# Two attention mixers: a fill piece ahead of the scores, rotary swaps on ScalarE, output pieces in halves

## The reference, cut to what matters

```python
proj = xn @ w_in                      # q, k, v: 12 heads of 64; qm: 4 memory heads; layer 0 also f_logit
log_f = log_sigmoid(f_logit + b_forget)                        # layer 0
sc = q @ k.T * scale + cumsum(log_f)[q] - cumsum(log_f)[k]     # layer 0, causal

x1, x2 = split(x, 2, axis=-1)                                  # layer 1, q and k of each head
y = concatenate([x1 * cos - x2 * sin, x2 * cos + x1 * sin])    # rotary embedding
# layer 1: three dilated branches, joined by their log-sum-exp

mem_out = softmax(qm @ km.T * scale) @ vm                      # 4 heads over 256 memory tokens
h = h + merge_heads([mix, mem_out]) @ w_out
```

## Time and profile before

| what | value |
|---|---|
| median of 3 runs | 1809.51 us (1806.91 to 1810.58) |
| the profiled execution | 1806.99 us |
| its span in the trace | 1805.2 us |
| TensorE busy | 1759.5 us, 97% |
| VectorE, ScalarE, GpSimd busy | 940.4, 533.6, 1015.1 us |

### The profile page before, as it was taken

One profiled execution on the slowest core, in us unless ns is written; L12 is line 12 of the kernel. 1 busy time (PEld: TensorE's weight loads), 2 busy tenths in 40 slices (PEclk: granted clock), 3 DMA queues, 4 the chain that ended last, 5 costly groups with the idle time before them and its releaser, 6 DMA issues.

```text
span 1805.2 us, 24432 instructions
## 1 busy us (share of the span) xinstructions
PE 1759.5 (97%) x9567; PEld 1404.3 (78%) x9572; DVE 940.4 (52%) x1896; ACT 533.6 (30%) x1183; POOL 1015.1 (56%) x1046
## 2 busy tenths in 40 slices
PE   7999999999989999999999999999999999999998
PEld 6886678676668967779888888887677888888886
DVE  5976754695543355533663166335765356415642
ACT  3614534312542344423220012023664211101111
POOL 7533375554237744335777677756434577677762
PEclk9989999999999999999999999999999999999999
DMA  5220312230233321113332333222111233233331
GB/s 177 82 77 19 117 59 94 77 99 29 71 105 106 94 71 50 69 47 90 106 98 88 95 99 104 88 94 71 49 69 48 70 94 114 96 93 94 95 103 47
DMA packets 170994, 151.16 MB, mean 84 GB/s; under 512 B 5192, under 2 KB 145992, under 8 KB 170880
## 3 DMA queue, kind: packets, MB, share of 16 engines
q1 hardware_dynamic: 169280, 148.12, 26.8%
q10 hardware_dynamic: 1600, 1.48, 0.3%
HBM read 147.45 MB, written 2.14 MB: 83 GB/s over the span
## 4 chain that ended last, share of the span: by engine, by line
PE 93%; DVE 4%; ACT 2%; issue 1%; another core or an unknown queue 0%; DMA 0%; ACTq 0%; DVEq 0%
PE ps L281 77%; PE ps L1989 3%; PE ps L2022 2%; PE ps L2007 2%; PE ps L352 1%; PE ps L640 1%; PE ps L1486 1%; PE ps L1464 1%; PE ps L1995 1%; PE ps L1407 1%; PE ps L1415 1%; PE ps L665 1%; PE ps L1423 0%; PE ps L672 0%; PE ps L1476 0%
## 5 line engine op out<-in xcount | busy, mean ns | idle before, releaser
L127 POOL TENSOR_SCALAR w_hi<-w_raw 128x512 fp32r<-128x512 f32 x520 | 315.7, 635 | 747.0 <-PE ps L281 742.3
L131 POOL TENSOR_TENSOR w_lo<-w_raw,w_hi 128x512 fp32r<-128x512 f32 x520 | 694.5, 1367 | 11.3
L281 PE MATMUL ps<-x_hi,w_hi 128*128 128x512 f32 (+1 forms) x1448 | 538.0, 372 | 0.7 <-DVE x_lo L434 0.7
L281 PE MATMUL ps<-x_hi,w_lo 128*128 128x512 f32 (+1 forms) x1448 | 527.9, 365 | 0.0
L281 PE MATMUL ps<-x_lo,w_hi 128*128 128x512 f32 (+1 forms) x1448 | 527.9, 365 | 0.0
L281 PEld LDWEIGHTS ps<-x_hi,w_hi 128*128 128x128 f32 x1448 | 274.8, 190 | 69.0 <-issue 19.8
L281 PEld LDWEIGHTS ps<-x_hi,w_lo 128*128 128x128 f32 x1448 | 274.8, 190 | 43.7
L281 PEld LDWEIGHTS ps<-x_lo,w_hi 128*128 128x128 f32 x1448 | 275.1, 190 | 40.8 <-issue 0.5
L2291 DVE SCALAR_TENSOR_TENSOR ffn_cv<-ps,col,ffn_cv 128x510 f32<-128x510 f32 (+1 forms) x176 | 131.8, 749 | 192.3 <-ACT ffn_cv L2269 187.6
L2269 ACT ACTIVATE ffn_cv<-ps,col 128x512 f32<-128x512 f32 x88 | 63.8, 775 | 500.2 <-PE ps L281 500.2
L309 DVE TENSOR_TENSOR h<-h,ps 128x512 f32<-128x512 f32 x64 | 43.9, 687 | 261.4 <-PE ps L281 261.3
(11 more groups left out here) (346 smaller groups left out, 2394.1 us busy)
## 6 DMA issues: line engine op xcount, KB each, us to landing
w_raw<-w_up SPq DMA_DIRECT2D x88, 512.0 KB, 5.0
w_raw<-w_down SPq DMA_DIRECT2D x16, 1024.0 KB, 5.0
w_raw<-od_w_in SPq DMA_DIRECT2D x12, 1024.0 KB, 5.2
w_raw<-w_in_fox SPq DMA_DIRECT2D x10, 1024.0 KB, 5.3
w_raw<-w_in_dil SPq DMA_DIRECT2D x10, 1024.0 KB, 5.1
w_raw<-w_out SPq DMA_DIRECT2D x8, 1024.0 KB, 5.0
w_raw<-ev_w_in SPq DMA_DIRECT2D x7, 1024.0 KB, 5.3
w_raw<-w_down SPq DMA_DIRECT2D x8, 768.0 KB, 4.5
```

What stands on the lines that cost most here:

```text
L127: ins = pool.tensor_scalar(hi[:, c:min(c + PIECE, size)], raw[:, c:min(c + PIECE, size)], 1.0, 1.0, ALU.mult, ALU.mult)
L131: ins = pool.tensor_tensor(lo[:, c:min(c + PIECE, size)], raw[:, c:min(c + PIECE, size)], hi[:, c:min(c + PIECE, size)].bitcast(F32), ALU. ...
L281: mm = pe.matmul(o, l, r, start=start and i == 0, stop=stop and i == 2)
```

## The change

- Each fill piece runs one step earlier. Piece 0 runs ahead of step 0: in layer 0 before scores(0), in layer 1 behind scores(0). Ropes 4 to 11 and the evacuations of fill blocks move one step with them.
- The four swaps by TensorE in layer 1 and their permutation table are gone, with the table's load. ScalarE makes these swaps too. Behind the evacuations of blocks 1 to 4 it copies the rows of q0, k0, q1 and k1 from SBUF to bank 5.
- The first output parts of tiles 0 and 1, four k each in steps 28 and 29, are cut into halves of two k, in steps 27, 28, 29 and 30.

```diff
-                                step = [f[0] for f in self.fill].index(m) + 2
+                                step = [f[0] for f in self.fill].index(m) + 1
...
-                    for dst, src in ((self.cos, "c_rope_cos"), (self.sin, "c_rope_sin"), (self.swap, "c_rope_swap"),
-                                     (self.mask, "c_dilated")):
+                    for dst, src in ((self.cos, "c_rope_cos"), (self.sin, "c_rope_sin"), (self.mask, "c_dilated")):
...
             def tensor(self, pe):
-                def swap(i):
-                    dst, tile, m = self.rope_tiles[i]
-                    if i == 0:
-                        pe.wait_ge(self.tables_in, 64)
-                    pe.wait_ge(self.evacuated.s, self.evacuated.at(max(m, 1) + 1))
-                    if i >= 1:
-                        pe.wait_ge(self.swap_free, i)
-                    pe.matmul(ps[:, 5, :], self.swap[:, :], dst[:, tile, :], start=True, stop=True).then_inc(self.swapped, 1)
...
                 for m in range(4, self.prelude):
                     self.dense(pe, m, 0, KD)
-                    if layer == 1:
-                        swap(m - 4)
+                if layer == 0:
+                    self.dense(pe, *self.fill[0])
                 scores(0)
+                if layer == 1:
+                    self.dense(pe, *self.fill[0])
                 for s in range(self.N):
                     if s + 1 < self.N:
                         scores(s + 1)
-                    if s < len(self.fill):
-                        self.dense(pe, *self.fill[s])
-                    elif s == self.N - 4:
+                    if s + 1 < len(self.fill):
+                        self.dense(pe, *self.fill[s + 1])
+                    elif s == self.N - 5:
                         pe.wait_ge(W.split_done, out_.slots[0][0] + 1)
                         pe.wait_ge(self.freed.s, self.freed.at(6))
                         pe.wait_ge(self.evacuated.s, self.evacuated.at(len(self.blocks) - 1))
-                        out_.part(pe, 0, 0, 0)
+                        out_.part(pe, 0, 0, 0, (0, 1))
+                    elif s == self.N - 4:
+                        out_.part(pe, 0, 0, 0, (2, 3))
                     elif s == self.N - 3:
                         pe.wait_ge(self.evacuated.s, self.evacuated.at(len(self.blocks)))
-                        out_.part(pe, 0, 0, 1)
+                        out_.part(pe, 0, 0, 1, (0, 1))
+                    elif s == self.N - 2:
+                        out_.part(pe, 0, 0, 1, (2, 3))
...
             def scalar(self, act):
+                def swap(i, x):
+                    if i >= 1:
+                        act.wait_ge(self.swap_free, i)
+                    for q in range(4):
+                        ins = act.activation(ps[32 * q:32 * q + 32, 5, :], x[32 * (q ^ 1):32 * (q ^ 1) + 32, :], ACT.Copy,
+                                             scale=1.0 if q % 2 else -1.0)
+                    ins.then_inc(self.swapped, 1)
...
                 for m in range(self.prelude):
                     evacuate(m)
+                    if self.layer == 1 and 1 <= m < 5:
+                        dst, tile, made = self.rope_tiles[m - 1]
+                        act.wait_ge(self.evacuated.s, self.evacuated.at(max(made, 1) + 1))
+                        swap(m - 1, dst[:, tile, :])
                 probs(0)
...
-                    if s < len(self.fill) and self.fill[s][2] == KD:
-                        evacuate(self.fill[s][0])
+                    if s + 1 < len(self.fill) and self.fill[s + 1][2] == KD:
+                        evacuate(self.fill[s + 1][0])
                     copy(s)
...
             def vector(self, dve):
-                    if i < 4:
-                        dve.wait_ge(self.swapped, i + 1)
-                    else:
-                        dve.wait_ge(self.act_swapped, i - 3)
-                        dve.wait_ge(self.evacuated.s, self.evacuated.at(m + 1))
+                    dve.wait_ge(self.swapped, i + 1)
+                    dve.wait_ge(self.evacuated.s, self.evacuated.at(m + 1))
```

More of the change, by code:

```diff
@@ L1839, in __init__ @@
                     self.tmp, self.mask = at("rope_tmp", 44, [P, 2, S]), at("dilated_mask", 72, [P, S])
-                    self.cos, self.sin, self.swap = at("rope_cos", 74, [P, S]), at("rope_sin", 76, [P, S]), at("rope_swap", 78, [P, P])
-                    self.tables_in, self.swapped, self.act_swapped, self.swap_free, self.roped = (
-                        sem(n) for n in ("rope_in", "swapped", "act_swapped", "swap_free", "roped"))
+                    self.cos, self.sin = at("rope_cos", 74, [P, S]), at("rope_sin", 76, [P, S])
+                    self.tables_in, self.swapped, self.swap_free, self.roped = (sem(n) for n in ("rope_in", "swapped", "swap_free", "roped"))
                 n = 2 * self.N
@@ L2080, in evacuate @@
                         if m in self.turned_by_act:
[L2081 to L2085, removed]
+                            swap(self.turned_by_act[m], ps[:, bank, :])
                         act.activation(dst, ps[:, bank, 0:dst.shape[1]], ACT.Copy).then_inc(self.evacuated.s, 1)
@@ L2179, in vector @@
                 else:
-                    dve.wait_ge(self.tables_in, 64)
+                    dve.wait_ge(self.tables_in, 48)
                     for i in range(4):
@@ L2475, in constants @@
     cos, sin = (np.tile(g(ang).astype(f).T, (4, 1)) for g in (np.cos, np.sin))
-    swap = np.zeros((P, P), f)
-    for m in range(P):
-        swap[m + 32 if m % 64 < 32 else m - 32, m] = -1 if m % 64 < 32 else 1
     time4 = np.tile(np.arange(0, S, 4, dtype=f)[None, :], (P, 1))
@@ L2482, in constants @@
             "c_rope_cos": np.ascontiguousarray(cos), "c_rope_sin": np.ascontiguousarray(sin),
-            "c_rope_swap": swap, "c_time4": time4, "c_ident": np.eye(P, dtype=f)}
+            "c_time4": time4, "c_ident": np.eye(P, dtype=f)}
 def layouts(a):
```

## The result

The changed kernel takes 1795.04 us (median of 6 runs, 1791.04 to 1796.91), the kernel before 1809.02 (6 runs, 1806.91 to 1810.58): a ratio of 0.9921, 95% interval 0.9907 to 0.9935, so 14.0 us less where 9.3 were forecast, and outside the stated range. The changed kernel's profiled execution took 1796.79, 10.2 less than that of before. Most of this document is about the 4 us between these two distances: the profiled execution of before was 2.0 under the median of its kernel, that of the changed kernel 1.75 over its own.

What follows compares the result with a forecast made beforehand. TensorE, busy 97% of the span, was taken as the bound, so its work and waits count. 2.24 + 6.15 + 1.3 - 0.4 = 9.3 us, so 1809.5 - 9.3 = 1800.2, range over all cases 1796.5 to 1805.

Steps and rivals of the forecast that it cites:

- The granted clock is not in question: Layer 1's stretch with the longest wait, 1240.5 to 1244, has clock 1.00, the upper level; no gain by the clock counted.
- the profiled execution lay 2.5 below the median: Profiled execution 1806.99 against median 1809.5; the predicted time was taken from the median, 1809.5 - 9.3.
- Part 1: Layer 0: fill piece 0 ahead of scores(0) removes their wait for the forget sums; gain 2.24 us.
- Part 2: Layer 1's prelude: four swaps leave TensorE (3.45) and the wait for logits(0) goes (2.70); gain 6.15 us.
- The exclusive lock: Layer 1's ropes wait for whole GpSimd operations: rope 4.5, loss 2.1, 1802.3 us; chance 0.04 within the late-rope rival's 0.12.
- Part 3: Ropes 4 to 11 and evacuations one step earlier: cost 0; 2.8 us if a GpSimd split ran then.
- Part 4: Mixer ends, output parts in halves: gain 0.70 in layer 1, 0.6 in layer 0; 0.4 lost to four piece changes.
- all four: Rivals: late ropes 1801.1-1804.3 (0.12); joined steps or halves fail 1801.5-1803 (0.09); slow swaps 1814.5 (0.03); only swaps gained 1806 (0.03).

Runs made afterwards that it cites:

- e6: Kernel before with the fill one step earlier in layer 0 alone; swaps, layer 1 and whole output parts as before: 1805.26 us, ratio 0.9975.
- e4: Changed kernel with layer 1's first four swaps put back on TensorE as matmuls: 1797.92 us, ratio 0.9938 against the kernel before.
- e3: Changed kernel with the output parts of tiles 0 and 1 whole again: 1798.41 us, ratio 0.9936 against the kernel before.
- e1: Kernel before under a new name, no edit: 1808.33 us over 12 runs, ratio 0.9988.
- e7: Kernel before with only the first four swaps moved to ScalarE, fill and output parts as before: 1803.62 us, ratio 0.9976.
- e11: Changed kernel with fill piece 0 behind scores(0) in layer 0 too, bringing back the wait for cum: 1798.52 us, ratio 0.9949 against the kernel before.
- e12: Kernel before once more, unchanged, on the same chip as later runs of the changed kernel: 1808.71 us, ratio 0.9997.

## Why the prediction was wrong

- **The step that failed is the first: "The granted clock is not in question".** It rested on the earlier trace rows, one execution. That profile was the exception: of the three of the unchanged program it is the only one in which the clock fell in neither mixer. Filling the waits, with no work saved, is worth 3.3 us in the means (92 unchanged runs 1808.7, 23 with idle work 1805.5); the changed kernel's 17 runs have 1795.6. So the whole, 13.2, is about 3 by the clock and 10 by work and waits. The split is an estimate over chips: within the two groups that have both kernels, idle work was worth 3.7 and 2.4. The mixers, 10.2, agree with it, and so do the runs at one mean clock, 0.994: unchanged and changed are 10.5 apart (1807.0 and 1796.6).
- **Chance has a share in the 14.0.** The six runs behind it had a mean of 1794.7, three of them at a mean clock of 0.996 or 0.997; the changed kernel's eleven later runs have 1796.0, with medians of 1796.74 and 1795.48. The first of these lies within the forecast's range, the second a little outside. Since the clock fell in the mixers of none of its three profiles, their scatter most likely comes from outside the mixers.
- **A sign of it was in the text.** I noted that the profiled execution lay 2.5 below the median and carried it along as a constant. It was no constant: the profile was a fast execution, and what made it fast was in reach of the change.
- **Part 1** had 2.24; layer 0's mixer lost 2.29 with that part alone (e6). Right.
- **Part 2** had 3.45 and 2.70. The swaps are worth 3.42 (e4). What is left of layer 1's 7.02 after them and the 1.01 of the halves is 2.59. Right; the chain of swaps and ropes ended 1.4 ahead instead of 1.0. The exclusive lock of the Trainium skill ("SBUF — State Buffer", "SBUF: two separate sides") would have made a rope of 4.5; the four took 2.4 to 3.75, so operations were held up, the longest, 1.67 instead of 0.68, by 0.99, but none by the full 1.27.
- **Part 3**, cost nothing: TensorE has no wait in steps 5 to 24.
- **Part 4** is the mis-sized term: 1.3 less 0.4 was forecast, 1.9 came (e3). The cutting cost what I took (0.35, all in layer 1). What I had at nothing is that a wait costs more than its row: the next 12 matmuls take 0.26 longer, in both tails, so 0.5. Another 0.2 is at the `values` of step 28 in layer 1: with whole parts no piece stands between scores and them, and they come 0.15 later and take 2.38 instead of 2.31. The rest, 0.2 to 0.3, I can't name.
- The sum by work was thus short by about 1, the clock's part by about 3. No rival had either; all four gave times above the forecast.

The Trainium skill ("TensorE: Matmul & The Clock Gate", "Why this matters for your kernels") tells that idle gaps bring the lower clock back. By the length that it names, the waits here would be harmless. The profiles of e1, e6, e7, e11 and e12 show the lower clock behind waits of 1.6 to 2.7, so the measurement decides.

Left open: why the clock falls in one execution and not in the next, and why the stretch at half clock is twice as long in layer 0 of e1 and e12 as in e7 and e11, behind the same wait. All fourteen profiles also have a lower clock somewhere from 75 to 104 us, outside the mixers; what brings it, and whether the waits outside the mixers can be filled, was not tried. No variant beat the changed kernel.

## What to carry to other kernels

A wait of a few microseconds on a busy TensorE can cost twice, once as idle time and once, in some executions, as half clock behind it. One profile doesn't show that: compare its time with the median, and if it is the faster, ask which stretches had full clock by luck. A wait that can't be removed can be filled with matmuls that nobody reads, and that is also the cheapest test of whether the clock plays a part.

## What the runs showed of the hardware

- Waits of TensorE of 1.6 to 2.7 us in the mixers were followed by the lower level (0.50) in 8 of 11 cases, at 1.5 to 2.7 us each; 17 mixers without such a wait had none. Outside the mixers, waits of 1.9 to 2.4 were followed by it in 17 of 56 cases.
- A stretch at 0.50 of 6.8 us cost 2.6 to 2.7, one of 3.4 cost 1.5 to 1.6.
- Twelve matmuls of 512 columns behind the last transposes take 3.06 with a wait of 0.7 between and 2.80 without one; behind scores of layer 1 they take 2.96 to 3.00 without any wait.
- ScalarE copies 32x512 between shifted partitions in 0.59 out of SBUF and 0.56 out of PSUM.
